# Attention units of block 2's mixers set 2.75 steps of the table apart in place of 2.5

## The chip, the cores and the metric

The kernel runs on one core of a Trainium2 chip. The metric is the device time of one execution in microseconds; several executions are taken and their median is given. TensorE multiplies, VectorE, ScalarE and GpSimd work on elements, and each of the five engines (SyncE issues most DMAs) runs its own list of instructions in order. Engines meet only in semaphores.

## The reference

A model of two blocks on 512 tokens of width 1024, in float32. Block 1 (two layers) isn't touched by the change. Block 2 has two layers of a mixer, a cross attention to a memory of 256 rows, and an MLP, each with a layer norm. Cut to the mixer:

```python
def hybrid_mixer(x, positions, w_in, conv_w, rel_bias, w_out):
    proj = jnp.einsum('bsd,dp->bsp', x, w_in)
    (cb, cc, ch, dq, dk, dv, iq, ik, iw, cq, ck, cv) = jnp.split(proj, offs, axis=-1)
    y_conv = short_conv_mixer(cb, cc, ch, conv_w)
    # dq, dk, iq, ik get a partial rotation by position
    y_dsa = dsa_attention(dq, dk, dv, iq, ik, iw)      # keys chosen by a top 128 of index scores
    y_chk = chunk_band_attention(cq, ck, cv, rel_bias)  # keys of the last 8 chunks of 64, plus a bias
    return jnp.einsum('bsm,md->bsd', jnp.concatenate([y_conv, y_dsa, y_chk], axis=-1), w_out)
```

Both attentions have six heads of 64, with a softmax over the allowed keys.

## The kernel before

Activations lie feature-major, 128 features to a tile. Every weight piece (128x1024) is loaded by SyncE into one of three staging buffers, split by ScalarE into a high part (line 1163) and by VectorE into a low part (line 1729), and TensorE forms each product as three matmuls, high x high, low x high and high x low (lines 574, 577, 580; for the token-major products 671, 673, 677).

A mixer is written as a table of steps. Steps 16 to 91 are the 19 tiles of the projection `w_in2`, four steps a tile, two of the eight chunks a step, so six matmuls of 512 columns. Steps 92 to 107 are `w_mv`, the values of the memory for the cross attention, again six such matmuls a step. Then comes `w_mix`, the output projection, whose chunks are taken in the order MIX_ORDER (line 274), the sparse attention's chunks 2, 3 and 4 last. All engines walk the same table, each in its own function, and what stands beside the tile's matmuls is set by tables of step numbers:

- UNITS2 (line 267) has 24 attention units, numbered 0 to 23. A unit is one pair of heads and one block i of 128 queries, with (i+1)*128 keys. Units 0 to 11 are of the chunk attention ("c", pair by pair, i from 3 down to 0), 12 to 23 of the sparse attention ("d", i from 0 up to 3, three pairs each).
- A unit at step s: TensorE's scores at s (line 906, for "d" also the mask's matmul, line 912), ahead of the step's six matmuls; VectorE's bias addition (2135) and maximum (2139) at s; ScalarE's exponentials at s+1 (1428); VectorE's reciprocal at s+2 (2121), and behind it GpSimd's scaling (2524), in place, once per head; TensorE's transposes at s+3 (923), behind the six matmuls; ScalarE's copy of them at s+3 (1470); TensorE's weighting with the values at s+4 (934); ScalarE's high part of the result at s+4 (1461) and VectorE's low part, called the residual pair in the text, at s+5 (2115).
- The scores of all units share banks 4 and 5, transposes and results banks 6 and 7.
- TOP_STEP (line 266): VectorE's top-k for the blocks 1, 2 and 3 in rounds of a maximum and a replacement (2166, 2168), one round a step, 16 rounds from steps 41, 57 and 73; the mask (2171) is written in the last. A "d" unit of block i waits for mask i.
- The rotated tiles dk, dq0, dq1, dq2 have a matmul of TensorE (947) at steps 57, 61, 65 and 69, and VectorE's product with the sine table (2145) in the same step and addition (2126) in the next.
- At 91 ScalarE copies the memory's high parts (1495), at 92 VectorE makes their low parts (2202); two convolution tiles have their work at 80 to 85 and 92 to 97 (GpSimd 2537, 2542, 2546; VectorE 2189, 2192). ScalarE takes the first half of `w_mv` out of psum at 100 and 101 (1509).
- VectorE's other work is one weight split in four steps, from step 92 on one in two.

In VectorE's function the order inside a step is: residual pair, reciprocal, addition of a rotation, bias and maximum, sine product, index sum, top-k round, convolution, low parts of the memory, weight split. In ScalarE's: exponentials, tile, index, high part, copy of the transposes, convolution, memory, weight split, copy of `w_mv`.

Of the kernel before, what the change touches and what calls it, by code (L numbers as in the profile page):

```python
# [224 lines left out]
def along(row, width):  # L225
    if width <= BANK:
# [37 lines left out]
ROPE2 = ("iq", "ik", "dk", "dq")  # L264
IDX_STEP = 32
TOP_STEP = {1: 41, 2: 57, 3: 73}
UNITS2 = ([("c", p, i, 37 + (5 * n) // 2) for n, (p, i) in enumerate((p, i) for p in range(3) for i in (3, 2, 1, 0))]
          + [("d", p, i, 67 + (5 * n) // 2) for n, (i, p) in enumerate((i, p) for i in range(4) for p in range(3))])
CONV_STEP = [END2["ch", 0] + 1, END2["ch", 1] + 1]
MEM_STEP = TOK_STEPS + 4 * len(ORDER2)  # L270
STEPS2 = 108
# [32 lines left out]
def at_steps(table):  # L304
    return {step: key for key, step in table.items()}


UNIT_AT1 = [{at: (u, h, i) for u, (h, i, at) in enumerate(units)} for units in UNITS1]
UNIT_AT2 = {at: (u, kind, p, i) for u, (kind, p, i, at) in enumerate(UNITS2)}
UNIT_ATX = {at: (u, h, i) for u, (h, i, at) in enumerate(UNITSX)}  # L310
HEAD_LAST1 = [{h: u for u, (h, i, at) in enumerate(units)} for units in UNITS1]
LAST_CHK = {p: u for u, (kind, p, i, at) in enumerate(UNITS2) if kind == "c"}
STAT_AT1, ROT_AT1, GATE_AT1 = at_steps(STAT1), at_steps(ROT1), at_steps(GATE1)
# [843 lines left out]
def split_hi(e, w, K, n):  # L1157
    if n < len(PIECES):
        w.wait_ge(*K.done(LANDED[n % STAGING], n))
        if n >= PARTS:  # L1160
            w.wait_ge(*K.done("product", n - PARTS))
        cols = K.piece(n).shape[-1]
        e.activation(K.parts(n)[0][:, 0:cols], K.staged(n)[:, 0:cols], ACT.Copy).then_inc(*K.did("hi", n))  # L1163
# [240 lines left out]
def scalar_mixers(e, w, K, l):  # L1404
# [11 lines left out]
    for s in range(TOK_STEPS, STEPS2 + 5):  # L1416
# [80 lines left out]
        if s % 4 == 0 and TOK_STEPS < s <= MEM_STEP:  # L1497
            split_hi(e, w, K, first + 4 + (s - TOK_STEPS) // 4 + 2)
        if s == UNITS2[3][3] + 2:
            for c in range(2):  # L1500
# [588 lines left out]
def make_bias(e, w, K, l, p, c):  # L2089

    m, did, done = K.m, K.did, K.done
    ap, far = K.bias(p, c), m["small"][5][:, 2 * (p % 2) + c:2 * (p % 2) + c + 1]
    w.wait_ge(*done(f"landed_bias{p % 2}{c}", l, p))
    e.tensor_copy(far, ap[:, 0:1]).then_inc(*did("far", l, p, c))
    w.wait_ge(*done("far", l, p, c))
    e.tensor_scalar(ap[:, :], ap[:, :], far, None, ALU.subtract).then_inc(*did("near", l, p, c))
    w.wait_ge(*done("near", l, p, c))
    e.memset(ap[0:CHUNK, 256 - CHUNK:256], -MASKED).then_inc(*did("bias", l, p, c))


def vector_mixers(e, w, K, l):
# [4 lines left out]
    for s in range(TOK_STEPS, STEPS2 + 2):  # L2106
# [71 lines left out]
        if s in (TOK_STEPS + 9, TOK_STEPS + 11):  # L2178
            p = (s - TOK_STEPS - 9) // 2
            make_bias(e, w, K, l, p, 0)  # L2180
            make_bias(e, w, K, l, p, 1)
        if s == UNITS2[3][3] + 6:
            make_bias(e, w, K, l, 2, 0)
# [640 lines left out]
```

## Time and profile before

| | us |
|---|---|
| median of 3 runs | 2900.57 |
| lowest and highest | 2897.63, 2902.85 |
| the profiled execution | 2901.96 |
| its span | 2900.2 |

| engine | busy us | share |
|---|---|---|
| TensorE matmul | 2799.6 | 97% |
| VectorE | 1662.2 | 57% |
| ScalarE | 1265.1 | 44% |
| GpSimd | 422.5 | 15% |

All rows are of the profiled execution. The span is from its first to its last instruction. The ends of matmuls are modelled, so a pause of TensorE is read best from the starts and from the idle time in brackets. The first mixer's table runs from about 1295 to 1532 us, the second's from about 2095 to 2331 us. A row of the timeline has the start, the length, the engine, the line, the operation with out<-in, and in brackets the idle time before it and what ended that.

### The profile page before, as it was taken

Reading aid. Unit: us, or ns where it says so; the run is one execution under the profiler, and the core shown is the slowest. Engines: PE = TensorE matmul, PEld = TensorE weight load, DVE = VectorE, ACT = ScalarE, POOL = GpSimd, SP = SyncE. Lnnn points to the kernel's source line nnn. Section 1 sums busy time; section 2 is a strip of 40 time slices with the busy share of each in tenths; the row PEclk is TensorE's granted clock in tenths of the full one; section 3 lists DMA queues with packets and bytes.
Section 4 is the critical chain, followed back from the end, with each engine's and each line's share of the span. In section 5 each row is a group of like instructions: output and inputs, shape, how many; then the busy total and the mean of one; then the engine's idle time right before and its main releaser. Section 6 shows DMA issues by size and latency. Waiting matters only on the chain.

```text
span 2900.2 us, 39185 instructions
## 1 busy us (share of the span) xinstructions
PE 2799.6 (97%) x15778; PEld 2358.5 (81%) x15782; DVE 1662.2 (57%) x2517; ACT 1265.1 (44%) x2157; POOL 422.5 (15%) x337
## 2 busy tenths in 40 slices
PE   8999999999989999999999999999999999999997
PEld 7878999998877788887668878888776688788886
DVE  5786545454776745445876456333659764663335
ACT  5574322234574422224554545333445545453333
POOL 2222000001222000001343120000313431200003
PEclk9999999999999999999999999999999999999999
DMA  4112232332112333332123223223221132233231
GB/s 144 51 45 66 88 95 84 95 93 80 52 45 66 99 94 95 102 99 81 55 67 124 87 66 95 95 95 99 83 77 62 66 123 87 67 95 94 95 100 68
DMA packets 71923, 244.36 MB, mean 84 GB/s; under 512 B 9152, under 2 KB 10816, under 8 KB 71744
## 3 DMA queue, kind: packets, MB, share of 16 engines
q1 hardware_dynamic: 66528, 235.50, 25.3%
q10 hardware_dynamic: 5216, 6.36, 0.7%
q8 instruction: 126, 2.06, 0.3%
q14 instruction: 53, 0.43, 0.1%
HBM read 239.73 MB, written 2.10 MB: 83 GB/s over the span
## 4 chain that ended last, share of the span: by engine, by line
PE 83%; DVE 11%; ACT 2%; issue 2%; POOL 1%; ACTq 0%; DVEq 0%
PE psum L574 23%; PE psum L580 23%; PE psum L577 23%; PE psum L645 2%; DVE temp L2168 2%; DVE small L2166 1%; PE psum L671 1%; PE psum L677 1%; PE psum L673 1%; DVE weights_hi_lo L1729 1%; PE psum L1068 1%; PE psum L1080 1%; PE psum L764 1%; DVE small L2139 1%; PE psum L906 0%
## 5 line engine op out<-in xcount | busy, mean ns | idle before, releaser
L574 PE MATMUL psum<-act_hi_lo,weights_hi_lo 128*128 128x264 f32 (+2 forms) x2544 | 775.5, 344 | 3.6 <-ACT temp L1270 2.8
L577 PE MATMUL psum<-act_hi_lo,weights_hi_lo 128*128 128x264 f32 (+2 forms) x2544 | 751.4, 334 | 1.9 <-DVE weights_hi_lo L1729 1.9
L580 PE MATMUL psum<-act_hi_lo,weights_hi_lo 128*128 128x264 f32 (+2 forms) x2544 | 752.6, 335 | 0.0
L1163 ACT ACTIVATE weights_hi_lo<-weights_float 128x1024 fp32r<-128x1024 f32 (+2 forms) x446 | 463.7, 1042 | 518.4 <-PE psum L580 449.3
L1729 DVE TENSOR_TENSOR weights_hi_lo<-weights_float,weights_hi_lo 128x1024 fp32r<-128x1024 f32 (+2 forms) x446 | 555.8, 1247 | 223.9 <-ACT weights_hi_lo L1163 222.7
L574 PE MATMUL psum<-hidden_hi_lo,weights_hi_lo 128*128 128x512 f32 (+2 forms) x1584 | 519.8, 358 | 3.1 <-DVE x_residual L1982 1.5
L580 PE MATMUL psum<-hidden_hi_lo,weights_hi_lo 128*128 128x512 f32 (+2 forms) x1584 | 511.8, 353 | 2.3 <-POOL hidden_hi_lo L1992 2.2
L577 PE MATMUL psum<-hidden_hi_lo,weights_hi_lo 128*128 128x512 f32 (+2 forms) x1584 | 511.0, 352 | 0.0
L574 PEld LDWEIGHTS psum<-act_hi_lo,weights_hi_lo 128*128 128x128 f32 x2544 | 440.3, 189 | 70.9 <-issue 17.7
L580 PEld LDWEIGHTS psum<-act_hi_lo,weights_hi_lo 128*128 128x128 f32 x2544 | 438.8, 188 | 48.3
L577 PEld LDWEIGHTS psum<-act_hi_lo,weights_hi_lo 128*128 128x128 f32 x2544 | 438.5, 188 | 48.6 <-issue 2.6
L574 PEld LDWEIGHTS psum<-hidden_hi_lo,weights_hi_lo 128*128 128x128 f32 x1584 | 280.0, 189 | 44.9 <-DVE x_residual L1982 2.1
L580 PEld LDWEIGHTS psum<-hidden_hi_lo,weights_hi_lo 128*128 128x128 f32 x1584 | 279.5, 189 | 43.6 <-POOL hidden_hi_lo L1992 2.8
L577 PEld LDWEIGHTS psum<-hidden_hi_lo,weights_hi_lo 128*128 128x128 f32 x1584 | 279.7, 189 | 39.0 <-issue 0.5
L1998 DVE SCALAR_TENSOR_TENSOR x_residual<-x_residual,psum 128x512 f32<-128x512 f32 (+1 forms) x108 | 74.6, 690 | 289.3 <-PE psum L580 289.3
L2524 POOL TENSOR_SCALAR temp<-temp,small 128x512 f32<-128x512 f32 (+3 forms) x96 | 108.4, 1141 | 206.8 <-DVE small L2121 206.7
L2389 DVE TENSOR_TENSOR hidden_hi_lo<-temp,hidden_hi_lo 128x512 fp32r<-128x512 f32 x52 | 36.0, 692 | 172.2 <-ACT hidden_hi_lo L1659 172.2
L1375 ACT ACTIVATE hidden_hi_lo<-temp 128x528 fp32r<-128x528 f32 (+1 forms) x44 | 28.1, 639 | 201.7 <-DVE temp L2034 201.7
L2554 POOL TENSOR_TENSOR act_hi_lo<-x_residual 128x512 fp32r<-128x512 f32 x4 | 8.9, 2227 | 733.1 <-DVE x_residual L1998 733.1
L2469 POOL TENSOR_TENSOR temp<-temp 128x528 f32<-128x528 f32 (+1 forms) x24 | 38.2, 1593 | 436.4 <-ACT temp L1206 435.9
L1688 ACT ACTIVATE temp<-psum 128x512 f32<-128x512 f32 x52 | 31.1, 598 | 136.5 <-PE psum L580 136.5
L1370 ACT ACTIVATE temp<-temp 128x528 f32<-128x528 f32 (+1 forms) x44 | 28.1, 639 | 132.9 <-DVE temp L2022 132.9
(277 smaller groups left out, 3325.0 us busy)
## 6 DMA issues: line engine op xcount, KB each, us to landing
weights_float<-in_w_ff SPq DMA_DIRECT2D x128, 512.0 KB, 3.6
weights_float<-in_w_gu SPq DMA_DIRECT2D x88, 512.0 KB, 3.6
weights_float<-in_w_in SPq DMA_DIRECT2D x70, 512.0 KB, 3.7
weights_float<-in_w_down SPq DMA_DIRECT2D x32, 448.0 KB, 3.4
weights_float<-in_w_out SPq DMA_DIRECT2D x16, 512.0 KB, 3.6
weights_float<-in_w_down SPq DMA_DIRECT2D x16, 512.0 KB, 3.5
weights_float<-in_w_mv SPq DMA_DIRECT2D x16, 512.0 KB, 3.2
weights_float<-in_w_mix SPq DMA_DIRECT2D x16, 512.0 KB, 3.3
```

The costliest lines, as they stand in the source:

```text
L574: e.matmul(slot[:, place:place + c1 - c0], w_hi[:, col], x_hi[:, c0:c1], start=first, stop=False)
L577: e.matmul(slot[:, place:place + c1 - c0], w_lo[:, col], x_hi[:, c0:c1], start=False, stop=False)
L580: mm = e.matmul(slot[:, place:place + c1 - c0], w_hi[:, col], x_lo[:, c0:c1], start=False, stop=final)
L645: mm = e.matmul(slot[:, place:place + c1 - c0], weights, moving[:, c0:c1], start=first, stop=final)
L1163: e.activation(K.parts(n)[0][:, 0:cols], K.staged(n)[:, 0:cols], ACT.Copy).then_inc(*K.did("hi", n))
L1688: e.activation(raised(f), K.bank[2 * RING["w_ff1", l, f]], ACT.Relu).then_inc(*did("relu", l, f))
L1729: e.tensor_tensor(lo[:, 0:cols], K.staged(n)[:, 0:cols], hi[:, 0:cols].bitcast(F32), ALU.subtract).then_inc(*K.did("lo", n))
L1998: e.scalar_tensor_tensor(along(x, width), along(x, width), alpha, across(K.psum[slot], width), ALU.mult, ALU.add).then_inc(*K.did(*mark))
L2168: e.match_replace(score, best[:, 0:8], score, TAKEN).then_inc(*did("top", l, i, s, "taken"))
L2389: e.tensor_tensor(lo, raised(f), hi.bitcast(F32), ALU.subtract).then_inc(*did("hid_lo2", l, f))
L2469: e.tensor_tensor(total, total, K.sq1[k % 3][:, 0:width], ALU.add).then_inc(*K.did("square_sum", stage, l, k))
L2524: e.tensor_scalar(prob, prob, m["small"][u % 4][:, 6 + c:7 + c], None, ALU.mult).then_inc(*did("scaled", l, u, c))
```

## The change

The two lists of UNITS2 get another spacing. Before, the "c" units stand at 37, 39, 42, 44, 47, 49, 52, 54, 57, 59, 62, 64 and the "d" units at 67, 69, 72, 74, 77, 79, 82, 84, 87, 89, 92, 94. After, at 37, 39, 42, 45, 48, 50, 53, 56, 59, 61, 64, 67 and 70, 72, 75, 78, 81, 83, 86, 89, 92, 94, 97, 100. All that hangs on a unit's step goes with it in each engine's function. The reload and preparation of the bias of pair 2, which hang on the step of unit 3 (`UNITS2[3][3] + 2` at line 1499, `+ 6` at line 2182), go from 46 to 47 and from 50 to 51.

```diff
-UNITS2 = ([("c", p, i, 37 + (5 * n) // 2) for n, (p, i) in enumerate((p, i) for p in range(3) for i in (3, 2, 1, 0))]
-          + [("d", p, i, 67 + (5 * n) // 2) for n, (i, p) in enumerate((i, p) for i in range(4) for p in range(3))])
+UNITS2 = ([("c", p, i, 37 + (11 * n) // 4) for n, (p, i) in enumerate((p, i) for p in range(3) for i in (3, 2, 1, 0))]
+          + [("d", p, i, 70 + (11 * n) // 4) for n, (i, p) in enumerate((i, p) for i in range(4) for p in range(3))])
```

## Rows read from the trace of the kernel before

**Rows 1.** The page, busy time of the engines over the span.
```profile
PE 2799.6 (97%) x15778; PEld 2358.5 (81%) x15782; DVE 1662.2 (57%) x2517; ACT 1265.1 (44%) x2157; POOL 422.5 (15%) x337
```

**Rows 2.** TensorE's waits, 1295 to 1545 us: total, times, longest.
```profile
PE psum L923 <- POOL temp L2524: 6.3, 9, 1.6
PE psum L906 <- ACT temp L1428: 1.5, 4, 0.6
PE psum L923 <- DVE hidden_hi_lo L2115: 1.0, 2, 0.6
PE psum L671 <- ACT arena L1443: 1.0, 1, 1.0
PE psum L906 <- DVE select_masks L2171: 1.0, 1, 1.0
```

**Rows 3.** Busy time by stretch: length, engines (instructions), clock, DMA share, GB/s.
```profile
1330.00:1350.00 20.00, 20.00 (x87) 13.93 (x85) 10.60 (x23) 5.79 (x11) 1.31 (x1) 1.00 0.25 80
1450.00:1470.00 20.00, 18.62 (x105) 12.65 (x105) 19.31 (x45) 10.48 (x34) 7.03 (x8) 1.00 0.22 79
1470.00:1490.00 20.00, 17.83 (x108) 11.94 (x104) 19.34 (x39) 11.45 (x32) 7.18 (x7) 1.00 0.16 53
```

**Rows 4.** VectorE's timeline, waits for rotations; the last row is of the second mixer.
```profile
1420.82 0.69 DVE L2145 TENSOR_TENSOR temp<-psum,rope_tables 128x512 f32<-128x512 f32 x1 [3.69 <-PE psum L947]
...
1432.01 0.69 DVE L2145 TENSOR_TENSOR temp<-psum,rope_tables 128x512 f32<-128x512 f32 x1 [0.41 <-PE psum L947]
...
1442.40 0.69 DVE L2145 TENSOR_TENSOR temp<-psum,rope_tables 128x512 f32<-128x512 f32 x1 [1.02 <-PE psum L947]
...
2219.99 0.69 DVE L2145 TENSOR_TENSOR temp<-psum,rope_tables 128x512 f32<-128x512 f32 x1 [2.11 <-PE psum L947]
```

**Rows 5.** TensorE's timeline around step 60 of the first mixer, and one stretch.
```profile
1414.78 0.63 PE L923 MATMUL psum<-consts,temp 128*128 128x128 f32 x4 [1.57 <-POOL temp L2524]
1416.32 0.76 PE L923 MATMUL psum<-consts,temp 128*128 128x128 f32 x4 [0.91 <-POOL temp L2524]
...
1418.15 0.63 PE L574 MATMUL psum<-act_hi_lo,weights_hi_lo 128*128 128x512 f32 x1
1418.58 0.63 PE L577 MATMUL psum<-act_hi_lo,weights_hi_lo 128*128 128x512 f32 x1
...
1418.00:1420.00 2.00, 2.00 (x5) 1.38 (x5) 0.00 (x0) 1.04 (x1) 2.00 (x3) 0.50 0.62 187
```

**Rows 6.** VectorE's groups by shape, 1340 to 1530 us: count, busy us, mean ns.
```profile
L2115 DVE TENSOR_TENSOR hidden_hi_lo<-psum,hidden_hi_lo 64x128 fp32r<-64x128 f32 x48 | 13.7, 286 | 10.1 <-ACT hidden_hi_lo L1461 9.3
L2139 DVE TENSOR_REDUCE small<-psum 128x2 f32<-128x768 f32 x6 | 5.7, 957 | 0.2
L2121 DVE RECIPROCAL small<-small 128x2 f32<-128x2 f32 x24 | 3.8, 159 | 0.9 <-ACT temp L1428 0.4
```

**Rows 7.** VectorE's timeline, the end of step 88.
```profile
1486.79 0.69 DVE L2166 MAX8 small<-temp 128x8 f32<-128x512 f32 x1
...
1488.30 0.70 DVE L2166 MAX8 small<-temp 128x8 f32<-128x512 f32 x1
...
1489.82 0.43 DVE L2171 TENSOR_SCALAR select_masks<-temp 128x512 bf16<-128x512 f32 x1
```

**Rows 8.** GpSimd's timeline, scaling of a unit of 384 keys and of one of 512.
```profile
1491.06 2.47 POOL L2524 TENSOR_SCALAR temp<-temp,small 128x384 f32<-128x384 f32 x2 [4.62 <-DVE small L2121]
...
1506.04 3.11 POOL L2524 TENSOR_SCALAR temp<-temp,small 128x512 f32<-128x512 f32 x2 [3.10 <-DVE small L2121]
```

**Rows 9.** TensorE's timeline, steps 87 to 89; the unit has 384 keys.
```profile
1482.72 0.88 PE L934 MATMUL psum<-temp,arena 128*64 128x128 f32 x12
1483.53 0.92 PE L906 MATMUL psum<-arena 64*128 64x384 f32 x4
...
1484.58 0.53 PE L574 MATMUL psum<-act_hi_lo,weights_hi_lo 128*128 128x512 f32 x1
...
1486.11 0.98 PE L923 MATMUL psum<-consts,temp 128*128 128x128 f32 x6
1486.85 0.48 PE L574 MATMUL psum<-act_hi_lo,weights_hi_lo 128*128 128x512 f32 x1
...
1488.42 0.88 PE L934 MATMUL psum<-temp,arena 128*64 128x128 f32 x12
1490.30 1.13 PE L906 MATMUL psum<-arena 64*128 64x512 f32 x4 [1.01 <-DVE select_masks L2171]
```

**Rows 10.** TensorE's timeline, its waits for scaling behind step 92.
```profile
1509.29 0.63 PE L923 MATMUL psum<-consts,temp 128*128 128x128 f32 x4 [0.50 <-POOL temp L2524]
...
1515.18 0.63 PE L923 MATMUL psum<-consts,temp 128*128 128x128 f32 x4 [0.81 <-POOL temp L2524]
```

**Rows 11.** ScalarE's groups by shape, 1340 to 1530 us.
```profile
L1163 ACT ACTIVATE weights_hi_lo<-weights_float 128x1024 fp32r<-128x1024 f32 x23 | 24.3, 1056 | 5.7 <-PE psum L677 5.2 <-issue 0.3
L1428 ACT ACTIVATE temp<-psum,small 128x512 f32<-128x512 f32 x12 | 8.2, 689 | 5.5 <-DVE small L2139 5.5
```

## The prediction

> **What bounds the kernel now.** I read the page first: TensorE is shown busy 97% of 2900.2 us [rows 1], so a change can only win back idle or slowed TensorE time, or lose more. Only the two runs of block 2's mixers hold changed code. The sum of waits over the first of them says what there is to win there: 11.4 us, of which 6.3 wait for GpSimd's scaling of the probabilities (line 2524), and the rest in small pieces for the exponentials, for a bank that VectorE must read, for the third selection mask and for a psum copy [rows 2]. The second mixer has the same waits. So 23 us at most are in play, 0.8%.
>
> Who is behind GpSimd? In the tables by stretch, TensorE runs 87 matmuls in 20 us (0.23 us each) without a pause where few units stand, with VectorE at 10.6; between 1450 and 1490 VectorE is at 19.3 of 20 us and TensorE has holes [rows 3]. There VectorE runs the rounds of the third top-k, one per step. It is the bound of the steps from about 47 to 88, not through its sum but through order: GpSimd scales a unit when VectorE has done its reciprocal, two steps after the scores, and TensorE transposes one step later. Where VectorE itself waits in these steps, the time is lost to both: 3.69, 0.41 and 1.02 us before the three rotations of dq (steps 61, 65, 69), in the second mixer 2.11 for the first of them [rows 4]. That one is the largest hole: unit 8 (512 keys) stands at 57, its transposes at 60 wait 1.57 and 0.91 us for 3.1 us of scaling, and the rotation that VectorE needs is behind them. In the first mixer the granted clock was 0.50 after it (1.2 GHz in place of 2.4), with matmuls 0.43 us apart instead of 0.23 [rows 5]; in the second mixer it stayed at 1.00, and VectorE's wait is 1.58 us shorter.
>
> **The change, part by part.** Nothing is added or removed: 24 units a mixer, the same instructions on each engine. Units 3 to 23 go later by 1 to 6 steps; those with steps of 89 or more are 19 to 23 (89, 92, 94, 97, 100) where they were 21 to 23 (89, 92, 94). DMAs: the loads of two bias tiles on ScalarE's queue go from step 46 to 47 and make_bias from 50 to 51; their first reader goes from 57 to 59, and weight loads hang on TensorE's products alone. Both cost nothing.
>
> 1. VectorE's work up to step 88. It loses the reductions of units 19 and 20, 2 x 0.96, and one unit's residual pair, 2 x 0.29: 2.5 us with the rest of the last digit [rows 6]. The reciprocals that fall in the stretch from 47 on are as many as before. Saved: 2.6 us per mixer (bounds: 2.5, and 2.7 with one reciprocal of 0.16).
>
> 2. VectorE's waits. With unit 8 at 59 its transposes come at 62, behind the rotation of 61; that hole goes. But unit 9 (384 keys) goes to 61 and is transposed at 64, one step ahead of the rotation of 65. From its reciprocal VectorE has one residual pair, a bias addition, a reduction and two rounds of the top-k until it needs that rotation, about 4.5 us; TensorE has 2.47 us of scaling, a transpose group, six matmuls at 0.23 and the rotation, about 5.4: 0.9 us of wait. Unit 6 does the same to 57 for 0.3. Unit 10 (64, transposed at 67) keeps something like today's 1.02 before 69; I take 1.2. Sum 2.4, against 5.1 and 3.5 now [rows 4]: saved 2.7 in the first mixer, 1.1 in the second. Bounds: all of it saved (5.1 and 3.5), or nothing.
>
> 3. The step at which the top-k ends. Now unit 21's scores at 89 wait for the third mask [rows 2], so TensorE ends step 89 some 3.1 us after VectorE's step 88: 1.5 for the scores, 1.55 for the step's matmuls. After the change unit 21 stands at 94 and this wait is gone. What is late next is unit 18's transposes at 89: its reciprocal stands ahead of the last round (1.51 between starts) and the mask (0.43) of step 88 [rows 7], so 2.1 us before its end; 2.47 of scaling [rows 8], the last three transposes and the handing on bring TensorE to the end of step 89 about 1.0 us after VectorE's step 88. Saved: 2.1 us, on top of 1 and 2 (bounds 1.0, the wait alone, and 3.1).
>
> 4. What TensorE has to do after step 89 grows: the scores of a unit of 384 keys and of one of 512, one group of transposes and two of weightings. By the starts around step 87, scores take 1.05 us, transposes 0.74, a weighting 0.81 [rows 9]; the larger scores 1.5. 1.05 + 1.5 + 0.74 + 2 x 0.81 = 4.9, and 0.15 for the slower first matmul after each of four groups: 5.5 us. Bounds: 4.9, and 6.1 by the whole unit (two steps with one unit take 5.76, two bare steps 2.76, so 3.0 a unit). This work filled holes while VectorE held the pace; behind step 88 it has no hole to fill. It is the price of the change, and it is nearly what 1 to 3 save.
>
> 5. Late waits. Behind step 89 TensorE now waits 1.0 for a psum copy [rows 2] and 0.50 and 0.81 for scaling [rows 10]. After the change ScalarE's copies of the memory come a step earlier against TensorE's work, and the psum copy is in time, but VectorE's low parts then follow a reduction: 0.8 us. Unit 20 at 92 shares VectorE's steps with these low parts: 0.4. Units 21 and 22 have the next unit's scores between them and their transposes: none. Unit 23 at 100 is the bad one: ScalarE has the copies of unit 22's transposes, a weight split (1.06) and the first copy of the memory's values before its exponentials [rows 11], and VectorE then a residual pair before its reciprocal, so both of its transpose groups at 103 wait, 1.1 + 1.2 us. With two pauses before masked scores: 3.9 against 2.5, so 1.4 more. Neither a time of this kind nor the position exists in the trace; bounds: nothing more than now, and three large units at today's worst case of 2.48 us each [rows 5], 7.4 in place of my 2.3, which makes 6.5 of the 1.4. I take 1.4, since the nearest rows [rows 10] stand at the same spacing of table steps.
>
> Sum: first mixer -2.6 - 2.7 - 2.1 + 5.5 + 1.4 = -0.5; second -2.6 - 1.1 - 2.1 + 5.5 + 1.4 = +1.1. Together +0.6 us. The profiled execution took 2901.96 us (span 2900.2), 1.4 above the median of 2900.57, within the spread of the runs; a difference of 0.6 on the median gives 2901.2 us.
>
> Weighed against this: TensorE's clock was halved for some 3 us behind the hole at step 60 in the first mixer and not in the second [rows 5]. The Trainium skill, page "TensorE: Matmul & The Clock Gate", Part 1, says that a stretch in which TensorE idles drops its clock to 1.2 GHz and that sustained work brings it back, with a phase that differs between runs. The trace agrees with its 0.50. By that rule the change could take one fall away (at step 60) and set one at step 103 in both mixers.
>
> **The rivals.**
> - Slower: the late units. One mechanism: ScalarE copies unit u's transposes before the exponentials of unit u+1 wherever units stand three steps apart, and each large unit in the steps from 94 then waits for scaling. It decides from the point where that chain (copies, exponentials, reciprocal, 3.1 us of scaling) exceeds three steps. Price: +6.5 per mixer in place of +1.4 is 2911.4; with the clock at 1.2 GHz behind the last one, 1.6 more each (the 3.69 against 2.11 of [rows 4]): 2914.6. For: 3.1 us of scaling is 6.3 of today's waits. Against: only two such waits, of 0.5 and 0.8, among today's three late units.
> - Faster: all of VectorE's waits go and the late waits stay at 2.5. -2.6 - 5.1 - 2.1 + 5.5 = -4.3 and -2.6 - 3.5 - 2.1 + 5.5 = -2.7: 2893.6. For: unit 8's hole, the largest, is surely undone. Against: unit 9 takes its place ahead of the next rotation.
> - The wait only moves from 61 to 65 and 69, so part 2 is nothing: +2.3 per mixer, 2905.2.
> - It does nothing: VectorE's sum isn't what times these steps and the end stays where TensorE's own work puts it, 2900.6.
>
> **How the numbers follow.** Chances: forecast 0.44, slower rival 0.18, faster rival 0.20, the moved wait 0.12, nothing 0.06. The forecast's own range is 2897 to 2906, from the bounds of parts 3 and 4. Two tenths of a per cent (5.8 us, about what a measurement can tell here) is passed by most of the faster rival and by the slower one, and by a little of the others: faster 0.18, same 0.62, slower 0.20. The range of 8 in 10 takes in the price of the faster rival and the slower one up to its first price: 2893 to 2911.
>
> **What the changed profile would show.** Part 1 and 2: the last mask operation (line 2171, 512 keys) some 5 us earlier in the first mixer, counted from the mixer's first units, and the wait of line 2145 for line 947 at the first dq rotation gone, with about 1 us at each of the next two. Part 3: no wait of the scores for line 2171, and a wait of 1 to 2 us for line 2524 at unit 18. Part 4: the stretch from that mask to the last weighting longer by about 5. Part 5: two waits above 1 us for line 2524 at the last unit. It would be wrong if VectorE shows long waits in steps 47 to 88, or if more than one late unit waits over 1 us.

## The result: slower by 11 us, and the profile after

| | before | after |
|---|---|---|
| median, us | 2901.36 | 2912.37 |
| lowest and highest, us | 2897.63, 2904.32 | 2909.13, 2913.22 |
| profiled execution, its span, us | 2901.96, 2900.2 | 2912.38, 2910.6 |

Six runs of each: the ratio is 1.0037, with a 95% interval of 1.0024 to 1.0050. The change is slower by more than 0.2%. The forecast was 2901.2, 0.6 us above the median of 2900.57 that it started from and so hardly any change, with a range of 2893 to 2911. The time is 11 us above, and 1.4 us outside the range.

The page after, busy time by engine:

```profile
PE 2804.6 (96%) x15778; PEld 2357.0 (81%) x15782; DVE 1665.8 (57%) x2517; ACT 1264.7 (43%) x2157; POOL 421.7 (14%) x337
```

The same number of instructions, and TensorE is shown busy 5 us longer for them than in [rows 1]; the other 5 us are idle. From the start of step 36 to that of step 107 the two mixers take 3.7 and 6.8 us more. Outside these stretches the differences cancel: the changed kernel comes to the first step 36 1.4 us later, and it is 1.5 us shorter between the mixers, where the granted clock of the kernel before was 0.50 from about 1683 to 1686 us and that of the changed one was not.

TensorE's waits after, 1295 to 1545 us, against [rows 2] (total, number of times, longest):

```profile
PE psum L923 <- POOL temp L2524: 8.1, 13, 1.4
PE psum L906 <- ACT temp L1428: 4.2, 4, 1.5
PE psum L677 <- DVE act_hi_lo L2202: 0.7, 1, 0.7
PE psum L923 <- DVE hidden_hi_lo L2115: 0.7, 1, 0.7
```

The wait for the third mask is gone, as meant, and the one for the psum copy too. The transposes' wait for the scaling grew from 6.3 to 8.1, and the scores' wait for the exponentials from 1.5 to 4.2.

To see where the time goes I took the start of each step's first dense matmul, less that of step 36 (the last one ahead of any moved unit), to step 107. "Elapsed" is that time in us, "waits" the sum of the idle times in brackets in it, and "rest" is elapsed less waits. A "boundary" is a place where small work (scores, transposes, weighting, rotation, index) gives way to dense matmuls (of 512 columns, six a step). A "fall" is a group of dense matmuls that follow each other by 0.43 us in place of 0.23; the granted clock is 0.50 at each. Two numbers in a field are the first and the second mixer.

| kernel | elapsed | waits | rest | boundaries | falls |
|---|---|---|---|---|---|
| before | 183.5, 181.9 | 11.4, 11.5 | 172.1, 170.4 | 53 | 1, 0 |
| after | 187.2, 188.7 | 14.2, 14.0 | 173.0, 174.7 | 62 | 0, 1 |

A mixer without a fall takes 5.3 us more: 2.7 of waits, 2.6 of rest. Twice 5.3 is 10.6, against 10.4 between the spans. A fall costs 1.5 to 1.7 and both kernels have one, in different places. Against the kernel before (second mixer) the changed one stands at -2.2 at the start of step 62, +1.5 at 72, -1.4 at 84, -3.6 at 89, -3.3 at 94 to 99, +0.3 at 101, +3.9 at 103 and +5.3 at 107. (The first mixer of the changed kernel is compared, which has no fall.) The lead of 3.6 at step 89 is mostly put off: by then it has started two units fewer than the kernel before. So it gains little while VectorE sets the pace and pays it all back, and more, behind the last mask.

VectorE's waits for the rotations after, against the first three of [rows 4], and the end of its top-k, against [rows 7]:

```profile
1420.58 0.69 DVE L2145 TENSOR_TENSOR temp<-psum,rope_tables 128x512 f32<-128x512 f32 x1 [0.22 <-PE psum L947]
...
1431.49 0.69 DVE L2145 TENSOR_TENSOR temp<-psum,rope_tables 128x512 f32<-128x512 f32 x1 [1.25 <-PE psum L947]
...
1442.47 0.69 DVE L2145 TENSOR_TENSOR temp<-psum,rope_tables 128x512 f32<-128x512 f32 x1 [1.35 <-PE psum L947]
```

```profile
1485.08 0.69 DVE L2166 MAX8 small<-temp 128x8 f32<-128x512 f32 x1
1487.19 0.67 DVE L2166 MAX8 small<-temp 128x8 f32<-128x512 f32 x1
1488.69 0.76 DVE L2171 TENSOR_SCALAR select_masks<-temp 128x512 bf16<-128x512 f32 x1
```

The hole at the first rotation is gone, with 1.25 and 1.35 at the next two, close to the 0.9 and 1.2 of the working. But counted from the start of step 36 the mask starts only 2.5 us earlier in the first mixer, of which 1.6 are the fall that is gone, and 0.9 us earlier in the second.

VectorE's waits from 1340 to 1490, first of the kernel before, then after, show why:

```profile
DVE temp L2145 <- PE psum L947: 5.1, 3, 3.7
DVE psum L2135 <- PE psum L906: 4.0, 3, 3.2
DVE hidden_hi_lo L2115 <- ACT hidden_hi_lo L1461: 1.7, 2, 1.2
```

```profile
DVE psum L2135 <- PE psum L906: 4.4, 4, 3.2
DVE hidden_hi_lo L2115 <- ACT hidden_hi_lo L1461: 2.9, 4, 1.2
DVE temp L2145 <- PE psum L947: 2.8, 3, 1.3
```

Part of what the rotations give back, VectorE now waits for the scores of the next unit (2135) and for ScalarE's high parts of a result (2115). Between the scores of unit 8 and those of unit 9, ScalarE and then TensorE wait in turn (ScalarE's row first):

```profile
1415.58 0.69 ACT L1428 ACTIVATE temp<-psum,small 128x512 f32<-128x512 f32 x1 [1.34 <-DVE small L2139]
```

```profile
1417.17 0.92 PE L906 MATMUL psum<-arena 64*128 64x384 f32 x4 [1.48 <-ACT temp L1428]
```

Unit 8 (512 keys, step 59) and unit 9 (step 61) share the banks of the scores. VectorE is late with unit 8's maximum, the exponentials follow, and unit 9's scores wait 1.48. The same is seen at units 4 and 5 (1.27), 12 and 13 (0.84), 16 and 17 (0.56), all two steps apart. Two steps alone don't make such a wait: the same units 8 and 9 stood two steps apart in the kernel before, where the scores waited 0.18, and no pair of it waited more than 0.56. It takes a place at which VectorE is behind as well. The hole of step 60 was replaced by these four.

The last unit, at step 103:

```profile
1525.08 0.39 PE L677 MATMUL psum<-weights_hi_lo,act_hi_lo 128*128 128x512 f32 x1
1526.33 0.63 PE L923 MATMUL psum<-consts,temp 128*128 128x128 f32 x4 [0.87 <-POOL temp L2524]
1528.39 0.63 PE L923 MATMUL psum<-consts,temp 128*128 128x128 f32 x4 [1.43 <-POOL temp L2524]
1528.77 0.47 PE L671 MATMUL psum<-weights_hi_lo,act_hi_lo 128*128 128x512 f32 x1
1529.08 0.39 PE L673 MATMUL psum<-weights_hi_lo,act_hi_lo 128*128 128x512 f32 x1
```

2.3 us of waits, as forecast (1.1 and 1.2). The two heads of this unit were scaled in 1.57 and 2.08 us, where [rows 8] has 3.11 for both, so 0.5 of the second wait comes from there. In the second mixer the clock fell behind them:

```profile
2332.50:2335.00 2.50, 2.50 (x10) 1.56 (x11) 0.00 (x0) 0.16 (x1) 0.00 (x0) 0.50 0.00 0
```

One thing of the table must be put more exactly than above, as it bears on all late units. Up to step 91 a unit's transposes stand behind the matmuls of their step. From step 92 on all small work stands ahead of the step's matmuls (`before()` at line 658), also the transposes. So a unit that starts at 89 or later has three steps of dense matmuls, 18, between its scores and its transposes, and an earlier one has four, 24. The kernel before has three such units (89, 92, 94), the changed one five (89, 92, 94, 97, 100).

### The profile page after: what moved, and what is told of

Its sections match the earlier page's. It is cut to its first block, busy times and chain, and to the rows that moved or that the text cites. A ratio compares the mean times of both kernels' runs of the same rounds, so it can differ in the third digit from the quotient of the medians.

```text
span 2910.6 us, 39185 instructions
## 1 busy us (share of the span) xinstructions
PE 2804.6 (96%) x15778; PEld 2357.0 (81%) x15782; DVE 1665.8 (57%) x2517; ACT 1264.7 (43%) x2157; POOL 421.7 (14%) x337
## 4 chain that ended last, share of the span: by engine, by line
PE 84%; DVE 10%; ACT 3%; issue 1%; POOL 1%; ACTq 0%; DVEq 0%
PE psum L574 23%; PE psum L580 23%; PE psum L577 23%; PE psum L645 2%; DVE temp L2168 1%; PE psum L671 1%; PE psum L677 1%; PE psum L673 1%; DVE weights_hi_lo L1729 1%; DVE small L2166 1%; PE psum L1068 1%; PE psum L1080 1%; POOL temp L2524 1%; PE psum L906 1%; PE psum L959 1%
## 5 line engine op out<-in xcount | busy, mean ns | idle before, releaser
L2389 DVE TENSOR_TENSOR hidden_hi_lo<-temp,hidden_hi_lo 128x512 fp32r<-128x512 f32 x52 | 36.0, 692 | 172.2 <-ACT hidden_hi_lo L1659 172.2
```

Source lines behind the costliest of these rows:

```text
L2389: e.tensor_tensor(lo, raised(f), hi.bitcast(F32), ALU.subtract).then_inc(*did("hid_lo2", l, f))
```

## The experiments

Every experiment runs all of the kernel's work. Line numbers are two higher in the first four. Each ratio is against the kernel before on the same chip. The code shown is cut; where it is a list of steps, the rest of the edit only writes that list out. First all of them in the terms of the table above:

| run | median | ratio, 95% interval | elapsed | waits | rest | boundaries | falls |
|---|---|---|---|---|---|---|---|
| e1_tail_late | 2909.26 | 1.0025, 1.0015 to 1.0035 | 186.6, 186.8 | 12.3, 12.4 | 174.3, 174.4 | 55 | 2, 2 |
| e2_head_late | 2906.63 | 1.0016, 1.0007 to 1.0026 | 185.1, 185.1 | 13.2, 13.3 | 171.9, 171.8 | 58 | 0, 0 |
| e3_copy_late | 2910.64 | 1.0032, 1.0022 to 1.0043 | 186.8, 188.4 | 13.9, 13.7 | 172.9, 174.7 | 62 | 0, 1 |
| e4_last_only | 2912.31 | 1.0033, 1.0020 to 1.0047 | 189.1, 186.3 | 15.5, 15.5 | 173.6, 170.8 | 53 | 2, 0 |
| e5_split_cluster | 2903.49 | 1.0006, 0.9996 to 1.0015 | 182.5, 184.1 | 8.1, 8.2 | 174.4, 175.9 | 75 | 0, 1 |
| e6_shift3 | 2907.94 | 1.0022, 1.0013 to 1.0032 | 187.5, 186.3 | 12.3, 12.3 | 175.1, 173.9 | 55 | 3, 2 |
| e7_unit8_early | 2902.68 | 1.0007, 0.9997 to 1.0017 | 182.3, 183.8 | 11.4, 11.3 | 170.8, 172.5 | 54 | 0, 1 |
| e8_memory_early | 2902.21 | 1.0006, 0.9997 to 1.0015 | 183.2, 183.3 | 11.0, 11.0 | 172.2, 172.3 | 53 | 1, 1 |
| e9_changed_split | 2916.38 | 1.0055, 1.0042 to 1.0069 | 190.0, 191.2 | 11.8, 11.8 | 178.2, 179.4 | 75 | 1, 2 |
| e10_split_where_late | 2899.07 | 0.9993, 0.9984 to 1.0002 | 180.8, 180.8 | 8.9, 9.0 | 171.9, 171.8 | 58 | 0, 0 |
| e11_two_cures | 2897.14 | 0.9981, 0.9972 to 0.9990 | 180.7, 180.7 | 8.5, 8.5 | 172.3, 172.2 | 59 | 0, 0 |
| e12_three_cures | 2896.90 | 0.9980, 0.9972 to 0.9989 | 180.6, 180.5 | 8.1, 8.1 | 172.5, 172.4 | 59 | 0, 0 |

**The last units alone.** Units 0 to 18 as before, 19 to 23 as changed.

```diff
-67, 69, 72, 74, 77, 79, 82, 84, 87, 89, 92, 94
+67, 69, 72, 74, 77, 79, 82, 89, 92, 94, 97, 100
```

> The spacing of before for units 0 to 18, the last five units where the change has them (89, 92, 94, 97, 100). Theory A (the tail): the price of the change is TensorE's work and waits of units 19 to 23 behind the third mask (step 88), +8 us a mixer from step 90 on, against 2 to 3 saved ahead of it; so nearly the whole loss is here, +4 to +6 us a mixer, 2909 to 2914 us in all. Theory B (the spacing): the loss comes from VectorE and ScalarE waiting for one another at the wider spacing of units 3 to 18, and the tail is cheap: within 2 us a mixer of before, 2899 to 2905 us.

Its first mixer takes 3.1 us more than the first of the kernel before, which has one fall to its two; with 1.6 taken off for each fall it is 1.5 more. So the median lies in theory A's range only by the falls, and the price without them is within theory B's 2 us. The last unit's waits at step 103 are 0.87 and 1.43, as after. In both mixers one of the falls came behind 1.84 and 0.70 us of waits at step 85, which were 0.76 and 0.70 before: there unit 18 is transposed, and unit 19, whose scores stood between, had gone to 89.

**The early units alone.** Chunk units as changed, the sparse ones squeezed so that the end stays at 94.

```diff
-67, 69, 72, 74, 77, 79, 82, 84, 87, 89, 92, 94
+70, 72, 74, 76, 78, 80, 82, 84, 87, 89, 92, 94
```

> The wider spacing of the chunk units (37 to 67) kept, the sparse units squeezed to 70, 72, 74, 76, 78, 80, 82, 84, 87, 89, 92, 94, so that they end as before. Theory A: as many units behind step 88 as before, so no price; what is left is the head's own gain or loss of about 1 us a mixer: 2899 to 2905 us. Theory B: the head's waits stay, +3 us a mixer or more: 2907 us or more.

3.2 us more per mixer, as theory B has it, though the median is just below its 2907. Against the second mixer of the kernel before it stands at -0.3 at step 74 and at +3.3 from 86 on; between these every pair stands two steps apart, and the units that the wider spacing had put off are caught up with. Its first mixer's waits:

```profile
PE psum L908 <- ACT temp L1430: 5.5, 5, 1.5
PE psum L925 <- POOL temp L2526: 4.0, 7, 0.8
```

The scores' wait for the exponentials is 5.5 as against 1.5 before, in five places, each with its pair two steps apart: 1.27, 1.48 and 0.85 as in the changed kernel, and 1.04 and 0.85 at steps 78 and 82. The other 1.4 us are rest, with five boundaries more. The hole of step 60 and the late units are both absent here, and the kernel is still slower.

**The changed kernel without the copies in the way.** ScalarE's copies of the memory's values out of psum go from steps 100, 101, 108, 109 to 103, 104, 109, 110.

```diff
-        if MEM_STEP + 8 <= s < STEPS2 + 4 and (s - MEM_STEP) % 8 in (0, 1):
-            half, i = divmod(s - MEM_STEP - 8, 8)
+        if s - MEM_STEP in (11, 12, 17, 18):
+            half, i = divmod(s - MEM_STEP - 11, 6)
```

> The changed kernel with ScalarE's four copies of the memory's values out of psum taken at 103, 104, 109 and 110 in place of 100, 101, 108 and 109. Theory A says that unit 23's two waits of 0.87 and 1.43 us hang on ScalarE's list between the scores at 100 and its exponentials at 101, of which the copy is 0.6: TensorE's waits for scaling at step 103 shrink by 0.5 to 0.7 us a mixer, about 1 us in all, and the clock may stay up behind them. If instead GpSimd's 3.1 us of scaling alone sets them, nothing changes.

The waits at step 103 went from 0.87 and 1.43 to 0.38 and 1.62, 0.3 us less per mixer. That is less than theory A's 0.5 to 0.7 and more than nothing. Counted from the start of step 100 the scaling begins 0.48 us earlier, and 0.19 of this is lost again, because the scaling of both heads takes 3.81 us where it took 3.62.

**One late unit.** The kernel before, unit 23 at 100 in place of 94.

> The kernel before with unit 23 alone moved from 94 to 100. Its work was behind step 88 already, so by theory A only waits change: the 0.81 us of today's last wait against the 2.3 of the changed kernel's, +0 to +2 us a mixer, 2901 to 2905 us. If lateness of the last unit costs by itself (its result is needed by the output projection), it is more: +3 us a mixer or above.

4.4 us more per mixer without a fall, nearly as much as the whole change, with the same number of boundaries and 4.0 us more of waits. The first theory had at most 2. The size is that of the second, but its reason isn't what the rows show: the time is lost in waits at steps 95 and 103, ahead of the output projection. TensorE's timeline of the first mixer:

```profile
1510.31 0.63 PE L925 MATMUL psum<-consts,temp 128*128 128x128 f32 x4 [1.48 <-POOL temp L2526]
1512.54 0.63 PE L925 MATMUL psum<-consts,temp 128*128 128x128 f32 x4 [1.60 <-POOL temp L2526]
...
1527.62 0.63 PE L925 MATMUL psum<-consts,temp 128*128 128x128 f32 x4 [0.67 <-POOL temp L2526]
1529.88 0.63 PE L925 MATMUL psum<-consts,temp 128*128 128x128 f32 x4 [1.63 <-POOL temp L2526]
```

Unit 22 wasn't moved, and yet its transposes at step 95 wait 3.1 us where they waited 0.50 [rows 10]. Two things add up to that. Unit 23's scores stood between, and without them TensorE is at the start of step 94 1.4 us earlier. And GpSimd's scaling of unit 22, which starts at the same time as before, takes 1.1 us longer than the 3.11 of [rows 8]:

```profile
1508.18 4.21 POOL L2526 TENSOR_SCALAR temp<-temp,small 128x512 f32<-128x512 f32 x2 [3.10 <-DVE small L2123]
```

Beside it VectorE now runs the convolution's two additions (2191, 2194), which in the kernel before stood behind the maximum of unit 23, and then a weight split. No run tells which of them slows it: single heads beside a weight split or beside these additions took 1.57 too. Three steps of dense matmuls alone are 4.1 us (18 at 0.23), and the chain from the scores of a unit of 512 keys over maximum, exponentials and reciprocal to the scaled probabilities is longer, as the waits show. Unit 23 waits 2.3 us at step 103, here with no unit near it and in the changed kernel with unit 22 three steps ahead; two steps behind unit 22 it waited 0.81 [rows 10].

**What a boundary costs.** The kernel before, with the scores between the two dense chunks of a step.

```diff
-        step(s)
...
         for k in (2 * quarter, 2 * quarter + 1):
+            step(s) if k % 2 else None
```

> The kernel before, with one change of order in steps 16 to 91: the small TensorE work that is due before a step's dense matmuls (the scores of a unit that starts there) is issued between the two dense chunks of the step, and no longer directly behind the small work that closed the step before. No operation is added or left out. In the kernel before, the weighting of one unit and the scores of the next but one touch; here a dense chunk stands between them, so that each mixer has some 20 more places at which small work gives way to dense work. Theory (a boundary between dense and small TensorE work costs about 0.3 us, worked out from 8 more boundaries and 2.6 us more non-idle time in the changed kernel): +4 to +6 us of non-idle time per mixer, +8 to +12 us in all. Rival (the changed kernel's extra non-idle time has to do with where its units stand and not with their clusters): within 2 us of the kernel before. Waits may move either way, since the scores come some 0.6 us later; they are read apart from the non-idle time.

22 more boundaries, 4.0 us more of rest (174.4 against 170.4), 0.18 each where 0.3 was expected; and 3.3 us less of waits, so the sum is only 0.6 more. The rows show where the 0.18 lie:

```profile
1483.88 0.39 PE L577 MATMUL psum<-act_hi_lo,weights_hi_lo 128*128 128x512 f32 x1
1484.10 0.40 PE L580 MATMUL psum<-act_hi_lo,weights_hi_lo 128*128 128x512 f32 x1
1484.43 0.88 PE L934 MATMUL psum<-temp,arena 128*64 128x128 f32 x12
1485.23 0.50 PE L574 MATMUL psum<-act_hi_lo,weights_hi_lo 128*128 128x512 f32 x1
1485.57 0.39 PE L577 MATMUL psum<-act_hi_lo,weights_hi_lo 128*128 128x512 f32 x1
1485.80 0.40 PE L580 MATMUL psum<-act_hi_lo,weights_hi_lo 128*128 128x512 f32 x1
```

From start to start a dense matmul takes 0.23; the last ahead of small work takes 0.33 and the first behind it 0.34. In the kernel before this weighting was followed by the scores at once, 1482.72 and 1483.53 in [rows 9].

**A late end alone.** All sparse units three steps later, spacing 2.5 kept.

```diff
-67, 69, 72, 74, 77, 79, 82, 84, 87, 89, 92, 94
+70, 72, 75, 77, 80, 82, 85, 87, 90, 92, 95, 97
```

> The kernel before with the twelve sparse units three steps later (70, 72, 75, 77, 80, 82, 85, 87, 90, 92, 95, 97) and the twelve chunk units where they were: same spacing of two and three steps, a later end. Theory (the loss of the changed kernel is its uneven spacing, which separates units' clusters, and its last unit that stands alone over bare steps): here the clusters still touch and the last unit has neighbours two and three steps before it, so within 2 us per mixer of the kernel before, 2900 to 2906 us in all, and the two waits of the last unit at step 100 to 101 stay under 1.6 us together. Rival (a late end by itself costs, about 1.5 us for each step that the last unit moves): +3 to +5 us per mixer, 2908 to 2912 us in all.

2907.94 and +4.4 us per mixer: the rival's price per mixer, with a median at the lower edge of its range of 2908 to 2912. But the table splits it: in the second mixer 0.8 of waits and 3.5 of rest with two boundaries more, and the rest holds two falls. The end itself was harmless: the last unit, two steps behind the one before it, waits 0.5 at step 100, and from step 93 on nothing else waits longer. The falls came behind holes at the end of step 88 and at the start of step 92 (second mixer):

```profile
2288.80 0.52 PE L923 MATMUL psum<-consts,temp 128*128 128x128 f32 x3 [1.24 <-POOL temp L2524]
2290.02 0.52 PE L923 MATMUL psum<-consts,temp 128*128 128x128 f32 x3 [0.70 <-POOL temp L2524]
2290.29 0.48 PE L574 MATMUL psum<-act_hi_lo,weights_hi_lo 128*128 128x512 f32 x1
...
2291.25 0.63 PE L574 MATMUL psum<-act_hi_lo,weights_hi_lo 128*128 128x512 f32 x1
2291.68 0.63 PE L577 MATMUL psum<-act_hi_lo,weights_hi_lo 128*128 128x512 f32 x1
...
2303.25 0.50 PE L671 MATMUL psum<-weights_hi_lo,act_hi_lo 128*128 128x512 f32 x1 [1.89 <-ACT arena L1443]
```

At the usual 1.5 to 1.6 a fall, 1.3 us per mixer remain, which is the theory's "within 2". Neither theory had the falls.

**Unit 8 one step earlier** (56 in place of 57), the pair behind the hole of step 60.

> The kernel before with one unit moved: unit 8 starts at step 56 in place of 57, so that three steps and not two lie between it and unit 9. Theory (the longest wait of TensorE in the middle of a mixer, at step 60 in the kernel before, and the fall of the clock behind it in the first mixer, come from that pair alone, and their removal is all that the changed kernel gains there): 1 to 2.5 us less per mixer, and no fall of the clock at steps 61 and 62: 2896 to 2900 us. Rival (the wait moves to another pair, as it does in the changed kernel): within 1 us of the kernel before, with new waits of 0.5 to 1.5 us beside the pair of units 7 and 8.

The rival holds. Unit 8's waits, now at step 59, went from 1.60 and 0.91 to 0.62 and 0.92, the wait of unit 11's scores at 64 went from 0.56 to 1.66, and the sum is 11.4 as before. In the second mixer the clock fell behind the 1.66 us at step 64; the kernel before had its fall behind step 60, in the first.

**The memory's high parts one step earlier** (step 90).

```diff
-        if s == MEM_STEP - 1:
+        if s == MEM_STEP - 2:
```

> The kernel before with one group of operations one step earlier: ScalarE's copies of the high parts of the memory input stand in step 90 in place of 91. Theory (TensorE waits 1.0 us for the last of them at the start of the memory matmuls, and nothing else comes late there): 1 us less per mixer, 2899 to 2901 us. Rival (ScalarE is as late with the exponentials that the copies now stand ahead of, and TensorE waits for those): within 0.3 us of the kernel before.

0.3 us less per mixer (183.2 against 183.5, both with a fall): the 1.0 us wait for the copy went, 0.7 for VectorE's low parts (2202) came. That is the rival's size, for another reason than the one it gave. The median shows nothing.

**The changed kernel with split clusters.** The edit of e5 on the changed kernel.

> The changed kernel, with the scores of a starting unit issued between the two dense chunks of its step, as in the run that split the clusters of the kernel before (which had 22 more boundaries per mixer, 4.0 us more of non-idle time, 0.18 each, and 3.3 us less of waits). In the changed kernel 11 of 22 unit pairs are apart already, so it gets fewer new boundaries. Theory (the changed kernel's extra non-idle time is that of its boundaries): 11 to 14 more boundaries at 0.18, so +2.0 to +2.5 us of non-idle time per mixer, which brings it to that of the kernel before with split clusters, 174.4 us, within 1 us. The scores' waits for the exponentials (4.2 us per mixer in four places) go, the other waits stay: -3 to -4. Sum -0.5 to -2 us per mixer against the changed kernel, 2908 to 2911 us. Rival (the extra time belongs to the later units themselves): the non-idle time ends 2 us or more above that of the kernel before with split clusters, and the whole at 2912 us or above.

The rival holds: without its fall the first mixer's rest is 176.6, 2.2 above that of e5 with the same number of boundaries. So boundaries are not all of it: something in where the units stand adds to the rest too. Against the changed kernel there are 13 more boundaries and 3.6 us more of rest, 0.28 each, and 2.4 us less of waits, not 3 to 4.

**Scores later only where they were late** (steps 54, 64, 72, 74, 89), the kernel before otherwise.

```diff
+            step(s) if (k % 2 == 1) == (s in (54, 64, 72, 74, 89)) else None
```

> The kernel before, with the scores issued between the dense chunks in five steps only (54, 64, 72, 74 and 89), those at whose start TensorE waits for exponentials, rotated parts or the last mask: 0.41, 0.56, 0.29, 0.36 and 1.03 us, 2.65 us per mixer. Theory (a dense chunk between the clusters costs 0.18 and gives the late operand 0.7 us more): 2.65 less 5 x 0.18, so 1.5 to 2 us less per mixer, 2898 to 2900 us against 2902. Rival (the time comes back as later waits for the same chains, because these set the end of the mixer and TensorE has slack against them): within 0.5 us per mixer, 2901 to 2903 us.

The median is in the theory's range, the gain per mixer between the two: the waits fell by 2.5 us per mixer as expected, the rest grew by 1.4 with five boundaries, and 1.1 us is left. The ratio's interval holds 1, so the medians show no gain clear of noise.

**That and unit 8 at 56; then the memory copies too.**

> The kernel before with two edits that were each tried alone: unit 8 starts at step 56 in place of 57, and in steps 54, 64, 72, 74 and 89 the scores stand between the two dense chunks. Alone, the first turned the 1.60 and 0.91 us of waits at step 60 into 0.62 and 0.92, but lengthened the wait at step 64 for unit 11's exponentials from 0.56 to 1.66; the second takes just that wait away, and left the hole at step 60. Theory (the two add up because each removes what the other leaves): 1.0 us less of waits than the second edit alone, 7.9 to 8.2 us per mixer against 8.9, no fall of the clock in either mixer, 2896 to 2898 us. Rival (the wait moves on to a third place, as it did each time): waits of 8.7 us or more per mixer, 2899 to 2901 us.

> The same two edits, and ScalarE's high parts of the memory input in step 90 in place of 91. Alone, the third took 0.3 us off each mixer, though the wait that it removes was 1.0 us. Theory (its gain is the same here): 0.3 us less per mixer than without it, 2895.5 to 2897.5 us. Rival (the earlier copies now stand ahead of the exponentials of the units around the last mask, whose scores come later in step 89): 0 to 1 us more per mixer than without it.

TensorE's waits in the first mixer of the first of them, against [rows 2]:

```profile
PE psum L923 <- POOL temp L2524: 5.4, 9, 0.9
PE psum L671 <- ACT arena L1443: 1.0, 1, 1.0
PE psum L906 <- ACT temp L1428: 0.8, 1, 0.8
PE psum L923 <- DVE hidden_hi_lo L2115: 0.6, 1, 0.6
```

The medians are 2897.14 and 2896.90 against 2902.82: faster than the kernel before by 0.2%, with intervals that end at 0.9990 and 0.9989, and so faster than the changed one. In the profiled mixers, which have no fall, the first of them has no gain over e10: the waits are 8.5, above the theory's 8.2 and below the rival's 8.7, and the rest grew by as much as they fell. The third cure takes 0.2 us off a mixer where 0.3 was expected, too little for the medians to show. What moving unit 8 adds is perhaps that no wait is longer than 1.0 us and no two neighbouring ones longer than 1.5 together, so that the clock has less to fall behind; the highest of 11 runs is 2899.21, where e10, on another chip, has 2902.51. This is not shown, as neither kernel's profile has a fall.

## Why the prediction was wrong

Against the kernel before without a fall, per mixer, forecast and measured:

| step of the working | forecast | measured |
|---|---|---|
| 1 VectorE's work up to step 88 | -2.6 | -1.75 |
| 2 VectorE's waits (second mixer) | -1.1 | +0.8 |
| 3 from the mask to the start of step 90 | -2.1 | -1.8 |
| 4 TensorE's work behind step 89 | +5.5 | +6.3 |
| 5 late waits | +1.4 | +1.7 |
| sum | +1.1 | +5.3 |

1. Mis-sized. VectorE's time from one start to the next, less its waits, from the start of step 36 to the third mask sums to 129.86 before and 128.11 after. The reductions gave 2.1, the reciprocals and residual pairs 1.2 and the earlier masks 0.95. But the weight splits (1729), the index sums (2158) and the top-k replacements (2168), the same in number, took 2.7 us longer in their new company.

2. This step failed, and it is the largest error. Its own rows came out as worked (rotations 3.5 to 2.8 in the second mixer). What it left out is that VectorE and TensorE bound each other here through several hands: as one wait goes, VectorE waits for residual pairs (+1.1) and for scores (+0.4), and TensorE for exponentials (+2.7). The rival of the moved wait was right in kind and too low, because it let the wait move among the rotations only. The experiment with unit 8 shows it most simply: 1.0 us removed at step 60, 1.1 added at step 64, sum unchanged. With steps 1 and 2 the mask comes 0.9 us earlier where 3.7 was forecast: 2.8 of the 4.2 that are missing.

3. Right in place and nearly in size. No scores wait for the mask after. Unit 18's transposes, which were to wait 1 to 2 us there, wait 0.20.

4. Right as a mechanism, 0.8 too small and above its own bound of 6.1. The allowance was 0.15 for each of four groups. Counted, there are four more boundaries in that stretch at 0.18 to 0.28 us each; and two matmuls at the start of the memory's values stand 0.40 and 0.34 apart in place of 0.23, next to the wait for VectorE's low parts of the memory. Over the whole mixer the boundaries are the item that the working had only in this allowance: with a spacing of 2, 3, 2, 3 steps two units on stands always five steps on, so that the weighting of unit u (four steps behind its scores) is followed directly by the scores of unit u+2. With 2.75 that is so in 11 of 22 cases. Nine more boundaries are 1.6 us by the price of e5 and 2.5 by that of e9, of 2.6. So 0.1 to 1.0 us per mixer of rest are not accounted for, and the boundaries as the cause of the others are worked out, not shown: no run takes the nine away from the changed kernel, and e9 has 2.2 us more of rest than e5 with as many boundaries. I didn't find that in one class of instruction.

5. Right: the last unit's two waits are 0.87 and 1.43 for 1.1 and 1.2. The reason given was only partly so. Moving the copies of the memory's values is worth 0.3, and 0.5 comes from the longer scaling of the second head; the unit waits because its chain is longer than the three steps of dense matmuls that units from 89 on have, and two steps' distance from the unit before is what kept this to 0.5 to 0.8 (the kernel before, e6). For units 21 and 22 "none" was right, and the reason given, the next unit's scores, is what e4 took away: of the 2.6 us that this cost, 1.4 were the scores' time and 1.1 a slower scaling.

Clock: the forecast named one fall to be lost at step 60 and one to be had at step 103. Both happened in the profiled executions, the second in one mixer of two, at 1.6 and 1.7 us, and they cancel. That is luck of these two executions: the forecast had the second fall in both mixers. The slower rival's price, 2911.4, is near the measured time, but its mechanism, waits of every late unit, is not there: only unit 23 waits above 1 us. It is no confirmation.

In the first mixer the kernel before had its fall, so there the sum is -0.5 forecast and +3.7 measured, the same error of 4.2.

## What to carry to other kernels

Where two engines take turns in step, price the removal of a wait by what is late next on every engine of the ring, not only at the place of the wait; an edit of one unit, like that of unit 8, tells in one run where the wait goes. There it could be removed only together with the next one (e11). Work that is spread out is cut into more pieces, and each change between small and dense matmuls has a price of its own; count these boundaries beside the instructions. The last unit of a pipeline has no later work to cover its chain; keep it close to the one before it.

## What the runs showed of the hardware

- A dense matmul of 512 columns takes 0.23 us from start to start among its like, 0.29 to 0.33 as the last ahead of a group of small ones and 0.33 to 0.34 as the first behind it (steps 36 to 91 of before and e5). Over whole mixers a boundary came to 0.18 us (22 more, e5) up to 0.28 (13 more, e9, and 5 more, e2 and e10).
- In the tables of the mixers the granted clock fell to 0.50, the lower level of 1.2 GHz, only behind waits of TensorE, among them 1.60 and 0.91 us, 0.87 and 1.43, 1.84 and 0.70, 1.24 and 0.70, one of 1.89, one of 1.66. The same hole was followed by a fall in one mixer and not in the other, and those of 1.48 and 1.60 at step 95 of e4 by none in either mixer. The Trainium skill, page "TensorE: Matmul & The Clock Gate", Part 1, describes such a drop behind an idle stretch and says that its phase differs between runs; these traces agree on both. The price in them is 1.2 to 1.8 us for a fall (e9 and e3, one mixer against the other).
- In a profile such a fall counts as busy time. Part of TensorE's longer busy time was this in several runs, and matmul starts and the granted clock told it from work.
- GpSimd's scaling of one head of 512 keys took 1.57 us nearly everywhere, but 2.08 for the second head of unit 23 in the changed kernel, 2.27 in e3, and 1.98 and 2.25 for the heads of unit 22 in e4, each with operations of VectorE beside it. What slows it is open.
